# V of a sample in one load of full rows, and the sample steps of the attention at other heads

## The chip, the cores and the metric

The kernel runs on all 8 cores of one Trainium2 chip. Each core has five engines with queues of their own: TensorE (PE, matrix products into PSUM), VectorE (DVE), ScalarE (ACT), GpSimd (POOL, here used for issuing DMAs that convert float32 to bfloat16) and SyncE (SP, which issues the other DMAs). They meet through semaphores alone. The metric is the device time of the slowest core, in microseconds (us), as the median of several runs.

## The reference, cut to what matters

A two-layer decoder trunk runs one step for a prompt group (8 sequences of 2048 tokens) and a sample group (128 sequences of one token, each with its own cached K and V of 256 memory rows). Both share all weights.

```python
def mem_attend(u, k, v, w_q, w_o):
    q = jnp.einsum('btd,de->bte', u, w_q).reshape(b, t, MEM_HEADS, MEM_HEAD_DIM)
    s = jnp.einsum('bthd,bnhd->bhtn', q, k).astype(jnp.float32) * (MEM_HEAD_DIM ** -0.5)
    p = jax.nn.softmax(s, axis=-1).astype(v.dtype)
    o = jnp.einsum('bhtn,bnhd->bthd', p, v).reshape(b, t, d)
    return jnp.einsum('btd,de->bte', o, w_o)
...
        x = x + y
        x = x + mem_attend(rmsnorm(x, g_attn[i]), mem_k[i], mem_v[i], w_q[i], w_o[i])
        x = x + sq_relu_mlp(rmsnorm(x, g_ffn[i]), w_up[i], w_down[i])
```

The width is 1024, there are 4 heads of 256, and 256 memory rows. The change is in `mem_attend` of the sample group, which is worked off inside the prompt group's attention.

## The kernel before, in words

Each core takes one prompt sequence (2048 tokens) and 16 samples, side by side as 2064 columns in five tiles: four of 416 columns and one, tile 4, of 384 prompt columns and the 16 samples. The order of instructions on each engine is the order in which the program is written; a tracker adds the semaphore waits that data, SBUF ranges and PSUM banks ask for. All helpers record on a line of their own: L284 is nearly every matrix product (`mm`), L301 an activation on ACT, L313 a scalar_tensor_tensor on DVE (here the products of a norm, x times gain times reciprocal root), L317 a tensor_tensor on DVE, L331 a copy on DVE, L329 a copy on ACT, L337 a multiply with a sum on DVE (the sample scores), L344 every DMA.

`layer` does the attention first. Its outer loop runs over k = 0..4, the tiles in the order `seq = [0, 4, 1, 2, 3]`; its inner loop runs over the heads h = 0..3, written here as (k, h). In a head stand `S` (scores of the next head, two PSUM banks, exponentials on ACT), a share of the list `big`, `PVh` (weights times V, three banks, normalised by two tensor_tensor on DVE) and the rest of that share. `big` holds `Qgroup(k+1, ec)`, eight products for one 128-column group of Q of the next tile, copied out by ACT, and `Ogroup`, eight products of the output map, added to x by DVE. Products take one of seven banks in turn (`nxt`), so a product waits until what was written seven allocations earlier has been read.

A norm of a tile to come (`norm_t`) stands after `PVh` of head 2 (of head 3 where k is 4): eight products with ones, two activations, and eight DVE products. Only the norm of k = 0 is deferred (`late_n`): its eight DVE products are let out two at a time by `norm_step(2)`, after each entry of `big` in k = 1, and `Qgroup(2, 0)`, the fifth entry there, reads their results.

The 16 samples are steps of a pipeline, one per call of `slot()`, made at the heads in the list `slots`, then once beside the last `Ogroup`s, then in the MLP. Call i runs `SE(i-1)` (exponential on ACT, a copy into a padded matrix on DVE), `SB(i-2)` (four products of 512 columns with V into bank 7), `SDV(i)` (loads V of sample i through POOL) and `SA(i)` (eight L337 on DVE: q times K, summed, for two K tiles of 128 memory rows). Each half of `SA` is followed by the load of a K tile into the buffer just read, `SDK`, three tiles ahead of it, so tile 2b+3 is asked for in the middle of `SA(b)` and read in the second half of `SA(b+1)`. q of the samples is made once, at (0, 2): `sample_q` turns it round on PE, stores it to memory (`qd`), and loads it back as a row repeated over all partitions (`SDQ`), two steps ahead.

At (3, 2) `wrelease_spread` starts a load of the first MLP down weights in eight pieces, one per head (`wspread_step`), on POOL's queue.

Of the kernel before, what the change touches and what calls it, by code (L numbers as in the profile page):

```python
# [8 lines left out]
BF16 = mybir.dt.bfloat16  # L9
# [4 lines left out]
PE, ACT, DVE, POOL, SP = "pe", "act", "dve", "pool", "sp"  # L14
NCORES = 8
D = 1024
# [8 lines left out]
PZM = 66  # L25
# [107 lines left out]
def build_program():  # L133
    nc = bass.Bass("TRN2", target_bir_lowering=False)
    P = Prog()

    def din(name, shape):
        return nc.dram_tensor(name, list(shape), F32, kind="ExternalInput").ap()
# [9 lines left out]
    cv_d = din("cv", [2, NS, NMEM, D])  # L148
# [29 lines left out]
    def DV(ap):  # L178
        return V(ap, [])
# [53 lines left out]
    def sl(a, b):  # L233
        return slice(a, b)

    def PSv(bank, a, b, m=128):
        return V(PS[0:m, bank, a:b], [(PSB + bank * 2048, PSB + (bank + 1) * 2048)], excl=True)
# [45 lines left out]
    def mm(out, lhsT, rhs, start, stop):  # L283
        P.add(PE, "c", lambda e, o=out.ap, l=lhsT.ap, r=rhs.ap: e.matmul(out=o, lhsT=l, rhs=r, start=start, stop=stop),  # L284
              [lhsT, rhs], [out])
# [57 lines left out]
    def dma(q, out, in_, chan, after=()):  # L343
        P.add(q, "d", lambda e, o=out.ap, i=in_.ap: e.dma_start(out=o, in_=i), [in_], [out], chan=chan, after=after)  # L344
# [497 lines left out]
    def layer(l, side=None, tail=None):  # L842
        fin = l == 1
        bank_mod[0] = 7
        s2 = Scratch2()
# [8 lines left out]
        so = s2.top  # L854
        assert so == ZOFF
        KS = [s2.alloc(F32, [D]) for _ in range(3)]
        VS = [s2.alloc(BF16, [2, 512]) for _ in range(4)]
        QB = [s2.alloc(BF16, [D]) for _ in range(2)]
        QS = QB[0]
        PZ = [s2.alloc(BF16, [4, PZW]) for _ in range(2)]  # L860
# [10 lines left out]
        def norm_t(ti, grow, defer=None):  # L871
            c0, n, npmt, ns = TILES[ti]
            norm_b(c0, n, grow, lambda c, c0=c0, n=n: U3(c, sl(c0, c0 + n)), SQ, RSTD, defer=defer)
# [60 lines left out]
                                       [(QDB + 8192 + l * 4096, QDB + 12288 + l * 4096)]), f"qb{b % 2}")  # L934

        def SDV(b):
            for hf in range(2):
                i = (2 * b + hf) % 4
                dma(POOL, VS[i](), DV(cv_d[l, b].rearrange("(nc p) e -> p nc e", p=128)[:, :, hf * 512:(hf + 1) * 512]), f"vs{i}")

        def SA(b):
            for ncx in range(2):
# [12 lines left out]
        def SB(b):  # L955
            for ncx in range(2):
                for hf in range(2):
                    w0 = 64 - (hf * 32 + 2 * b)
                    mm(PSv(7, 0, 512, m=PZM), PZ[b % 2](ncx * 2 + hf, sl(w0, w0 + PZM)), VS[(2 * b + hf) % 4](ncx),
                       b == 0 and ncx == 0 and hf == 0, b == NS - 1 and ncx == 1 and hf == 1)  # L960

        sctr = [0]
# [1 line left out]
        def slot():  # L964
            i = sctr[0]
            sctr[0] += 1
            if 0 <= i - 1 < NS:
                SE(i - 1)
            if 0 <= i - 2 < NS:
                SB(i - 2)  # L970
            if i < NS:
                SDV(i)
                SA(i)
# [28 lines left out]
        for ec in range(NCH):  # L1002
            Qgroup(0, ec)
            if ec == 3:
                norm_t(seq[1], R_ATTN + l)
        slots = [(0, 3), (1, 1), (1, 2), (1, 3), (2, 1), (2, 2), (2, 3), (3, 1), (3, 2), (3, 3), (4, 1), (4, 2)]
        late_n = []

        def norm_step(m):
# [193 lines left out]
    def tail0(j):  # L1203
# [7 lines left out]
        if j in (16, 18):  # L1211
            for half in range(2):
                conv.na((j - 16) // 2, half)
            conv.nb((j - 16) // 2)

    layer(0, side0, tail0)
    bank_mod[0] = 8
    conv.run()
    layer(1)

    sems = {e: es.enter_context(nc.semaphore(f"s_{e}")) for e in (PE, ACT, DVE, POOL)}
# [119 lines left out]
```

How the kernel before makes its waits and increments, by code:

```python
    def emit(name, e):  # L1230
        known = {}
        for op in P.q[name]:
            for d in op.cwaits:
                key = ("e", d.eng)
                if known.get(key, 0) < d.val:
                    e.wait_ge(sems[d.eng], d.val)
                    known[key] = d.val
            for ch, val in op.dwaits:
                key = ("c", ch)
                if known.get(key, 0) < val:
                    e.wait_ge(chans[ch], val)
                    known[key] = val
            ins = op.fn(e)
            if op.kind == "d":
                ins.then_inc(chans[op.chan], 16)
            elif op.sig:
                ins.then_inc(sems[name], 1)
        if name == SP:
            for ch, cnt in P.chan_count.items():
                if known.get(("c", ch), 0) < cnt * 16:
                    e.wait_ge(chans[ch], cnt * 16)
```

## Time and profile before

| | us |
|---|---|
| median of 3 runs | 1636.65 (1635.66 to 1760.3) |
| the profiled execution | 1635.83 |
| its slowest core, first to last instruction (core 4) | 1634.3 |
| its fastest core (core 7) | 1630.4 |
| PE busy on core 4 | 1589.7 |

The profile shows the slowest core of one execution; some 1.5 us lie around its span. PE busy counts stretches in which some matmul is in flight, so a PE at half clock counts as busy too. Layer 0's attention lies at about 95 to 260 us of the span, layer 1's at about 980 to 1137 us.

### The profile page before, as it was taken

What the parts mean: (1) busy time and instruction counts of PE and PEld (TensorE: products, weight loads), DVE (VectorE), ACT (ScalarE), POOL (GpSimd) and SP (SyncE); (2) the same over time, 40 slices, a digit from 0 to 9 for tenths busy, and PEclk for the clock granted to TensorE, in tenths of its full rate; (3) what the DMA queues carried; (4) which work ended last, traced back from release to release, by engine and by line L of the source; (5) the groups of instructions that cost most, each with busy time, mean ns of one, the idle gap of its engine ahead of it and who ended that gap; (6) DMA issues with size and microseconds to landing.
All of it is one profiled execution on the core that took longest, in us unless ns stands there. A gap on an engine that the chain in (4) does not pass through costs nothing.

```text
span 1634.3 us, 27613 instructions; the slowest of 8 cores (1630.4 to 1634.3 us)
## 1 busy us (share of the span) xinstructions
PE 1589.7 (97%) x9490; PEld 911.6 (56%) x9500; DVE 879.5 (54%) x1987; ACT 511.6 (31%) x988; POOL 80.4 (5%) x117
## 2 busy tenths in 40 slices
PE   6898999999999999999999999999999999999997
PEld 5654555555555555555555555555555555555565
DVE  5656577554443444456666572777744444444455
ACT  4755633221221221223222126553311122211234
POOL 0010121000000000000000000121100000000000
PEclk9999999999999999999999999999999999999999
DMA  9996998236307334114000067699406303303013
GB/s 246 195 206 117 211 186 184 73 53 103 59 7 123 66 64 73 32 26 79 1 1 1 1 92 145 155 209 220 112 14 104 52 1 52 52 1 53 21 65 125
DMA packets 70388, 146.20 MB, mean 89 GB/s; under 512 B 4414, under 2 KB 22078, under 8 KB 70236
## 3 DMA queue, kind: packets, MB, share of 16 engines
q0 software_dynamic: 47184, 76.21, 31.2%
q1 hardware_dynamic: 23068, 68.23, 13.5%
q8 instruction: 80, 1.31, 0.3%
q14 instruction: 56, 0.46, 0.1%
HBM read 207.18 MB, written 14.42 MB: 136 GB/s over the span
## 4 chain that ended last, share of the span: by engine, by line
PE 92%; DVE 3%; DMA 2%; ACT 2%; issue 1%; DVEq 0%; ACTq 0%; SPq 0%
PE PS L284 89%; DVE MEM L313 2%; PE PS L288 2%; PE PS L293 1%; ACT MEM L304 1%; DMA MEM<-ck 1%; ACT MEM L301 1%; DMA mn<-MEM 0%; DMA MEM<-qd 0%; DVE MEM L317 0%; DVE MEM L337 0%; DVE MEM L331 0%; ACT MEM L329 0%; DMA MEM<-gv 0%; DMA qd<-MEM 0%
## 5 line engine op out<-in xcount | busy, mean ns | idle before, releaser
L284 PE MATMUL PS<-MEM 128*128 128x416 bf16 (+4 forms) x8578 | 1520.4, 339 | 22.1 <-DVE MEM L317 8.4
L284 PEld LDWEIGHTS PS<-MEM 128*128 128x128 bf16 (+1 forms) x8588 | 841.1, 98 | 689.9 <-issue 35.7
L317 DVE TENSOR_TENSOR MEM<-PS,MEM 128x416 f32<-128x416 f32 (+5 forms) x601 | 339.4, 583 | 318.2 <-PE PS L284 266.7
L301 ACT ACTIVATE MEM<-PS 128x416 f32<-128x416 f32 (+3 forms) x465 | 233.8, 515 | 635.4 <-PE PS L284 537.5
L317 DVE TENSOR_TENSOR MEM<-MEM 128x416 bf16<-128x416 f32 (+1 forms) x320 | 186.4, 587 | 257.5 <-ACT MEM L301 257.5
L313 DVE SCALAR_TENSOR_TENSOR MEM<-MEM 128x416 bf16<-128x416 f32 (+5 forms) x314 | 192.0, 658 | 90.2 <-ACT MEM L301 85.2
L301 ACT ACTIVATE MEM<-MEM 128x1 f32<-128x1 f32 (+7 forms) x201 | 125.5, 633 | 97.1 <-DVE MEM L317 83.6
L337 DVE SCALAR_TENSOR_TENSOR MEM<-MEM 128x256 f32<-128x256 f32 x256 | 91.6, 419 | 20.6 <-DMA MEM<-ck 13.6
L329 ACT COPY MEM<-PS 128x416 f32<-128x416 f32 (+4 forms) x68 | 36.8, 543 | 178.8 <-PE PS L284 158.8
L329 ACT CAST MEM<-PS 128x416 bf16<-128x416 f32 (+3 forms) x101 | 51.9, 516 | 67.4 <-PE PS L284 55.7
L301 ACT ACTIVATE PS<-PS 128x416 f32<-128x416 f32 (+2 forms) x65 | 33.0, 507 | 92.2 <-PE PS L284 92.2
L344 POOL DMA_DIRECT2D MEM<-cv x64 | 44.9, 708 | 329.1 <-PE PS L284 328.7
L288 PE MATMUL PS<-MEM 128*128 128x128 bf16 (+3 forms) x640 | 45.9, 230 | 13.1 <-DVE MEM L313 8.3
L288 PEld LDWEIGHTS PS<-MEM 128*128 128x128 bf16 (+1 forms) x640 | 43.3, 112 | 16.3 <-issue 15.0
L313 DVE SCALAR_TENSOR_TENSOR MEM<-PS,MEM 128x1024 f32<-128x1024 f32 (+2 forms) x20 | 25.6, 1280 | 25.9 <-ACT MEM L301 25.9
L293 PE MATMUL PS<-MEM 128*128 128x128 f32 (+8 forms) x272 | 33.7, 265 | 0.7 <-DVE MEM L313 0.5
L293 PEld LDWEIGHTS PS<-MEM 128*128 128x128 f32 (+8 forms) x272 | 28.2, 130 | 7.5 <-issue 4.0
L304 ACT ACTIVATE MEM<-PS 128x1024 bf16<-128x1024 f32 (+2 forms) x20 | 20.4, 1018 | 34.5 <-PE PS L293 34.5
L344 POOL DMA_DIRECT2D MEM<-w_down x22 | 14.0, 650 | 313.4 <-PE PS L284 231.4
L331 DVE COPY MEM<-PS 128x512 f32<-128x512 f32 (+6 forms) x30 | 19.2, 663 | 15.7 <-PE PS L284 5.4
L304 ACT ACTIVATE MEM<-MEM 128x1024 bf16<-128x1024 f32 (+1 forms) x19 | 20.0, 1054 | 7.8 <-DMA MEM<-x 7.8
L331 DVE COPY MEM<-MEM 128x2 f32<-128x2 f32 (+2 forms) x120 | 15.9, 162 | 9.5 <-ACT MEM L301 9.3
(26 smaller groups left out, 86.5 us busy)
## 6 DMA issues: line engine op xcount, KB each, us to landing
MEM<-ck SPq DMA_DIRECT2D x64, 512.0 KB, 8.3
MEM<-w_up POOLq DMA_DIRECT2D x8, 2048.0 KB, 17.3
MEM<-cv POOLq DMA_DIRECT2D x64, 256.0 KB, 8.8
MEM<-w_down POOLq DMA_DIRECT2D x6, 2048.0 KB, 17.2
MEM<-x SPq DMA_DIRECT2D x16, 512.0 KB, 11.4
MEM<-w_kv POOLq DMA_DIRECT2D x4, 2048.0 KB, 30.2
MEM<-qd SPq DMA_DIRECT2D x32, 256.0 KB, 8.2
y<-MEM SPq DMA_DIRECT2D x15, 512.0 KB, 2.6
```

The lines of the kernel that those rows point to most:

```text
L284: P.add(PE, "c", lambda e, o=out.ap, l=lhsT.ap, r=rhs.ap: e.matmul(out=o, lhsT=l, rhs=r, start=start, stop=stop), [lhsT, rhs], [out])
L288: P.add(PE, "c", lambda e, o=out.ap, l=lhsT.ap, r=rhs.ap: e.matmul(out=o, lhsT=l, rhs=r, start=start, stop=stop, is_transpose=is_transpose ...
L293: P.add(PE, "c", lambda e, o=out.ap, i=in_.ap, d=ident.ap: e.transpose(out=o, in_=i, identity=d), [in_, ident], [out])
L301: P.add(ACT, "c", lambda e, o=out.ap, i=in_.ap: e.activation(out=o, in_=i, func=func, bias=bias, scale=sc), rd, [out])
L304: P.add(ACT, "c", lambda e, o=out.ap, i=in_.ap, c=acc.ap: e.activation(out=o, in_=i, func=func, bias=0.0, scale=1.0, accum_out=c), [in_], ...
L313: P.add(eng, "c", lambda e, o=out.ap, a=in0.ap, b=in1.ap: e.scalar_tensor_tensor(out=o, in0=a, scalar=sc, in1=b, op0=op0, op1=op1), rd, [out])
L317: P.add(eng, "c", lambda e, o=out.ap, a=in0.ap, b=in1.ap: e.tensor_tensor(out=o, in0=a, in1=b, op=op), [in0, in1], [out])
L329: P.add(ACT, "c", lambda e, o=out.ap, i=in_.ap: e.copy(out=o, in_=i), [in_], [out])
L331: P.add(eng, "c", lambda e, o=out.ap, i=in_.ap: e.tensor_copy(out=o, in_=i), [in_], [out])
L337: P.add(DVE, "c", lambda e, o=out.ap, a=in0.ap, b=in1.ap, c=acc.ap: e.scalar_tensor_tensor(out=o, in0=a, scalar=1.0, in1=b, op0=ALU.mult, ...
L344: P.add(q, "d", lambda e, o=out.ap, i=in_.ap: e.dma_start(out=o, in_=i), [in_], [out], chan=chan, after=after)
```

## The change

V of a sample was loaded in two DMAs of 512 columns each, into four buffers of 2 x 512; it is now loaded in one DMA of all 1024 columns, into two buffers of 2 x 1024. The memory used is the same, and V of samples i and i+1 are still held side by side. The list of heads that call `slot()` loses (0, 3), (1, 2), (2, 2) and (3, 2) and gains (1, 0), (2, 0), (3, 0) and (4, 0); it still has 12 entries.

```diff
-        VS = [s2.alloc(BF16, [2, 512]) for _ in range(4)]
+        VS = [s2.alloc(BF16, [2, D]) for _ in range(2)]
...
         def SDV(b):
-            for hf in range(2):
-                i = (2 * b + hf) % 4
-                dma(POOL, VS[i](), DV(cv_d[l, b].rearrange("(nc p) e -> p nc e", p=128)[:, :, hf * 512:(hf + 1) * 512]), f"vs{i}")
+            dma(POOL, VS[b % 2](), DV(cv_d[l, b].rearrange("(nc p) e -> p nc e", p=128)), f"vs{b % 2}")
...
-                    mm(PSv(7, 0, 512, m=PZM), PZ[b % 2](ncx * 2 + hf, sl(w0, w0 + PZM)), VS[(2 * b + hf) % 4](ncx),
+                    mm(PSv(7, 0, 512, m=PZM), PZ[b % 2](ncx * 2 + hf, sl(w0, w0 + PZM)), VS[b % 2](ncx, sl(hf * 512, (hf + 1) * 512)),
...
-        slots = [(0, 3), (1, 1), (1, 2), (1, 3), (2, 1), (2, 2), (2, 3), (3, 1), (3, 2), (3, 3), (4, 1), (4, 2)]
+        slots = [(k, h) for k in range(1, 5) for h in range(4) if h != (3 if k == 4 else 2)]
```

As steps, counted from 0: before, step 0 stood at (0, 3), steps 1 to 3 at heads 1, 2, 3 of k = 1, and so on to steps 10 and 11 at (4, 1) and (4, 2). Now steps 0 to 2 stand at heads 0, 1, 3 of k = 1, 3 to 5 at those of k = 2, 6 to 8 at those of k = 3, and 9 to 11 at heads 0, 1, 2 of k = 4. Steps 1, 4, 7, 10 and 11 stay where they were; the others come one head later.

On DVE, at the passage from k = 0 to k = 1 of a layer, before: the eight L317 are the normalisations of tile 0, L337 is `SA(0)`, each lone L317 of 128x416 with the pair of L313 behind it is one `Ogroup` addition and two products of the deferred norm, and the 128x384 are the normalisations of (1, 0).

```order
L317 TENSOR_TENSOR MEM<-PS,MEM 128x416 x8
L337 SCALAR_TENSOR_TENSOR MEM<-MEM 128x256 x8
L317 TENSOR_TENSOR MEM<-PS,MEM 128x416
L313 SCALAR_TENSOR_TENSOR MEM<-MEM 128x416 x2
L317 TENSOR_TENSOR MEM<-PS,MEM 128x384 x2
L317 TENSOR_TENSOR MEM<-PS,MEM 128x416
L313 SCALAR_TENSOR_TENSOR MEM<-MEM 128x416 x2
L317 TENSOR_TENSOR MEM<-PS,MEM 128x416
L313 SCALAR_TENSOR_TENSOR MEM<-MEM 128x416 x2
L317 TENSOR_TENSOR MEM<-PS,MEM 128x416
L313 SCALAR_TENSOR_TENSOR MEM<-MEM 128x416 x2
```

The same place on DVE now.

```order
L317 TENSOR_TENSOR MEM<-PS,MEM 128x416 x9
L313 SCALAR_TENSOR_TENSOR MEM<-MEM 128x416 x2
L317 TENSOR_TENSOR MEM<-PS,MEM 128x384 x2
L317 TENSOR_TENSOR MEM<-PS,MEM 128x416
L313 SCALAR_TENSOR_TENSOR MEM<-MEM 128x416 x2
L317 TENSOR_TENSOR MEM<-PS,MEM 128x416
L313 SCALAR_TENSOR_TENSOR MEM<-MEM 128x416 x2
L337 SCALAR_TENSOR_TENSOR MEM<-MEM 128x256 x8
L317 TENSOR_TENSOR MEM<-PS,MEM 128x416
L313 SCALAR_TENSOR_TENSOR MEM<-MEM 128x416 x2
```

`SA(0)` moved from ahead of all four pairs of norm products to a place between the third pair and the fourth.

On DVE, from the norm at (3, 2) to (4, 2), before: L313 x8 is that norm, L331 is the copy of `SE`, the three L337 rows are steps 9, 10 and 11 with step 8 ahead of them.

```order
L313 SCALAR_TENSOR_TENSOR MEM<-MEM 128x416 x8
L317 TENSOR_TENSOR MEM<-PS,MEM 128x416
L331 COPY MEM<-MEM 128x4x2
L337 SCALAR_TENSOR_TENSOR MEM<-MEM 128x256 x8
L317 TENSOR_TENSOR MEM<-PS,MEM 128x416 x5
L331 COPY MEM<-MEM 128x4x2
L337 SCALAR_TENSOR_TENSOR MEM<-MEM 128x256 x8
L317 TENSOR_TENSOR MEM<-PS,MEM 128x416 x10
L331 COPY MEM<-MEM 128x4x2
L337 SCALAR_TENSOR_TENSOR MEM<-MEM 128x256 x8
L317 TENSOR_TENSOR MEM<-PS,MEM 128x416 x5
```

The same place on DVE now.

```order
L313 SCALAR_TENSOR_TENSOR MEM<-MEM 128x416 x8
L317 TENSOR_TENSOR MEM<-PS,MEM 128x416 x6
L331 COPY MEM<-MEM 128x4x2
L337 SCALAR_TENSOR_TENSOR MEM<-MEM 128x256 x8
L317 TENSOR_TENSOR MEM<-PS,MEM 128x416 x5
L331 COPY MEM<-MEM 128x4x2
L337 SCALAR_TENSOR_TENSOR MEM<-MEM 128x256 x8
L317 TENSOR_TENSOR MEM<-PS,MEM 128x416 x5
L331 COPY MEM<-MEM 128x4x2
L337 SCALAR_TENSOR_TENSOR MEM<-MEM 128x256 x8
L317 TENSOR_TENSOR MEM<-PS,MEM 128x416 x5
```

Step 8 moved from one tensor_tensor behind the norm to six behind it, and step 9 into the stretch that had ten tensor_tensor in a row; in k = 4 three steps now stand five tensor_tensor apart.

## Rows read from the trace of the kernel before

**Rows 1.** The page: busy time of each engine, share of the span, instructions.

```profile
PE 1589.7 (97%) x9490; PEld 911.6 (56%) x9500; DVE 879.5 (54%) x1987; ACT 511.6 (31%) x988; POOL 80.4 (5%) x117
```

**Rows 2.** Span and mean granted clock of another core.

```profile
core 3: 1634.0 us, clock 0.994
```

**Rows 3.** Core 4, busy time by engine in stretches; then granted clock, DMA share, GB/s.

```profile
126.00:148.00 22.00, 17.44 (x93) 8.87 (x92) 13.38 (x36) 11.14 (x19) 0.00 (x0) 0.92 0.47 106
205.00:235.00 30.00, 27.47 (x146) 14.64 (x144) 21.03 (x71) 10.93 (x23) 5.21 (x9) 0.94 1.01 194
228.40:231.80 3.40, 3.40 (x12) 1.50 (x10) 1.95 (x4) 0.52 (x1) 0.00 (x0) 0.51 1.03 203
1005.00:1032.00 27.00, 22.88 (x133) 12.00 (x131) 15.15 (x42) 15.47 (x30) 0.00 (x0) 1.00 0.29 80
```

**Rows 4.** Core 4, timeline of layer 0's first heads; idle before and releaser in brackets.

```profile
129.57 0.33 SPq L344 DMA_DIRECT2D qd<-MEM  x1
...
134.09 0.49 ACT L301 ACTIVATE MEM<-PS 128x384 f32<-128x384 f32 x1
136.19 0.42 DVE L337 SCALAR_TENSOR_TENSOR MEM<-MEM 128x256 f32<-128x256 f32 x1 [4.31 <-DMA MEM<-qd]
...
138.97 0.58 DVE L317 TENSOR_TENSOR MEM<-PS,MEM 128x416 f32<-128x416 f32 x1
139.47 1.20 DVE L313 SCALAR_TENSOR_TENSOR MEM<-MEM 128x416 bf16<-128x416 f32 x2
...
139.70 5.63 PE L284 MATMUL PS<-MEM 128*128 128x384 bf16 x22 [3.21 <-DVE MEM L317]
...
146.62 18.55 PE L284 MATMUL PS<-MEM 128*128 128x416 bf16 x104 [0.23 <-DVE MEM L313]
```

**Rows 5.** Core 4, timeline of layer 1's first heads.

```profile
1013.40 0.33 SPq L344 DMA_DIRECT2D qd<-MEM  x1
...
1028.78 21.54 PE L284 MATMUL PS<-MEM 128*128 128x416 bf16 x121 [0.23 <-DVE MEM L313]
```

**Rows 6.** Core 3, timeline at the same two places and at (3, 3) of layer 0.

```profile
131.53 0.33 SPq L344 DMA_DIRECT2D qd<-MEM  x1
...
149.23 3.10 PE L284 MATMUL PS<-MEM 128*128 128x416 bf16 x17 [0.23 <-DVE MEM L313]
...
228.92 11.40 PE L284 MATMUL PS<-MEM 128*128 128x416 bf16 x63 [0.92 <-DVE MEM L317]
...
1012.72 0.33 SPq L344 DMA_DIRECT2D qd<-MEM  x1
...
1028.45 6.88 PE L284 MATMUL PS<-MEM 128*128 128x416 bf16 x39 [0.23 <-DVE MEM L313]
```

**Rows 7.** Core 4, timeline around (3, 3) of layer 0.

```profile
216.47 1.71 SPq L344 DMA_DIRECT2D MEM<-ck  x2
...
225.80 0.43 DVE L337 SCALAR_TENSOR_TENSOR MEM<-MEM 128x256 f32<-128x256 f32 x1 [4.08 <-DMA MEM<-ck]
...
227.92 9.39 PE L284 MATMUL PS<-MEM 128*128 128x416 bf16 x42 [2.53 <-DVE MEM L317]
```

**Rows 8.** K tiles from issue to landing, 205 to 250 us and 1085 to 1130 us.

```profile
DMA to landing us min/median/max: 6.2/9.6/11.3
DMA to landing us min/median/max: 5.8/8.1/10.7
```

**Rows 9.** DMA queues: 205 to 250 us (two rows), 1146 to 1180 us, 480 to 700 us.

```profile
q0 software_dynamic: 2863, 3.26, 57.1%
q1 hardware_dynamic: 1753, 5.36, 42.0%
q0 software_dynamic: 1992, 1.91, 37.9%
q0 software_dynamic: 6240, 12.58, 37.2%
```

## The prediction

> **What bounds the kernel now.** The page is read first: PE is busy for 1589.7 of 1634.3 us [rows 1], so nearly all time is matmul time, which the change leaves as it is. What can move is the 44.6 us in which PE does nothing, and stretches at half clock, which count as busy. The second view, PE's waits and the stretches by engine, says which of this lies where steps move. In 126 to 148 us of layer 0 PE is busy 17.44 of 22 us at a mean clock of 0.92; in 205 to 235 us 27.47 of 30 at 0.94; in 1005 to 1032 us 22.88 of 27 at 1.00 [rows 3]. The rest of the attention has no PE wait worth a term. So three places carry the sum, and together they are some 15 us, under one per cent.
>
> The third view, the timeline, tells why. At the first place `SA(0)` stands on DVE ahead of the `Ogroup` additions and of the deferred norm, and waits 4.31 us for the samples' q, which has just gone to memory and back. Behind it PE finds a bank whose addition is queued on DVE and stands for 3.21 us [rows 4]. It comes back to a steady run only at 146.62, when the last norm product lets `Qgroup(2, 0)` finish. Layer 1 has the same shape with a faster return of q [rows 5], and so has core 3 [rows 6]. At the second place, (3, 3) of layer 0, step 9 follows step 8 so closely that its second K tile, asked for at 216.47, is not there until 225.80; DVE waits 4.08 us, PE stands 2.53 us [rows 7] and then runs 3.4 us at a granted clock of 0.51, the lower of its two levels (1.2 of 2.4 GHz) [rows 3]. On core 3 this place costs 0.92 us [rows 6].
>
> **The change, part by part.** The sum is made for core 3, at 1634.0 us [rows 2], since core 4, at 1634.3, owes 4.2 us to the second place alone and falls behind it when that goes. The profiled execution took 1635.83, so 1.5 lie around the slowest span; it is 0.8 under the median of the runs shown.
>
> *Step 0 to (1, 0), first place.* From the end of `SA(0)` at 138.97 to the resumption of Q at 146.62 DVE works off four additions, four pairs of norm products and two normalisations: 7.65 us. An addition with its pair takes 0.50 and 1.20 [rows 4]. Now the first addition with its pair (1.7) fits into what was the wait for q, from 131.88 on. The normalisations of (1, 0) need the reciprocals, which end at 134.58 [rows 4]. From there the other 5.95 us and `SA(0)` itself, 2.78 (136.19 to 138.97), must pass before the last norm product, since `SA(0)` stands ahead of the last pair: 134.6 + 8.7 = 143.3. So Q resumes 13.75 us after the store of q at 129.57, where it took 17.05. q lands before `SA(0)` wants it, near 139. With 13.75 at all four places, core 4 gains 3.3 in layer 0 and 1.6 in layer 1, core 3 4.0 and 2.0 [rows 4 to 6]. Had `SA(0)` stood behind all eight products, it would be 2.8 us more each time; the list names heads that hold no norm, yet the deferred norm of k = 0 lies in head 0 and head 1 of k = 1.
>
> *The clock there.* PE will reach the seventh product of `Qgroup(2, 0)` some 2.4 us before DVE does. Standing still for 2.53 us was followed by a half-clock stretch of 3.4 us on core 4 [rows 3, 7], which costs 1.7; in layer 1 shorter pauses left it at 1.00 [rows 3]. So 0 to 3.4 for two layers; I take 1.7, since 2.4 is nearer to 2.53 than to the pauses that cost nothing.
>
> *Steps 2, 3, 5, 6, 8 and 9 one head later.* Each takes its `SE`, `SB`, V load and K loads along. A head of k = 1 or 2 with a step has 38 products (24 in groups, 4 of `S`, 6 of `PVh`, 4 of `SB`), at 18.55 / 104 = 0.178 us each [rows 4] 6.8 us. Step 9 no longer follows 8 within a few us, so the stall at (3, 3) goes: 0.9 on core 3, 2.5 and 1.7 of clock on core 4 [rows 3, 6, 7]. The norms at head 2 start with DVE free of a step; nothing on PE waited for them, so that is worth nothing.
>
> *What is late next: k = 4.* It gets three steps where it had two. DVE carries it: eight products of scores (2.8), a copy (0.2) and five tensor_tensor (2.6) are 5.6 us against PE's 6.8 per head. What does not carry it is DMA, which is full from 205 to 235 us (share 1.01) [rows 3]. Over 205 to 250 us 99% of 16 engines' time went into five steps and eight pieces of weights [rows 9]. A piece is 128 packets of 2 KB at 210 ns (37.2% of 220 us x 16 / 6240 [rows 9]), 1.7 us; so a step costs (44.6 - 13.4) / 5 = 6.2 us. Between the start of step 8 and the tile that step 11 reads last, steps 8 and 9, V and a K tile of step 10 and four pieces must move: 12.4 + 4.5 + 6.8 = 23.7 us. From (3, 3) to (4, 2) PE has 42 + 38 + 38 products, 21.1 us, and the first half of `SA(11)` adds 1.4. With the time that any K tile takes to land (5.8 at the least [rows 8], of which transfer is the smaller part), step 11 waits for K for 1 to 6 us. I take 4.0 in layer 0, the wait that the same crowding gave at (3, 3) [rows 7], and 2.5 in layer 1, where K lands 1.5 us sooner (8.1 against 9.6 in the median [rows 8]). Behind `SA(11)` on DVE are the addition of `Ogroup` 9, the normalisations of (4, 3) and the norm; PE has 42 products, 7.5 us, before it takes that addition's bank again. DVE's own share of that is 0.6 for the addition ahead, 3.0 for the step, 0.6 for the addition behind it and about 1.1 carried over from step 10, so it bears a wait of 2.2: PE stalls 1.8 and 0.5 us, together 2.3. Bounds: 0, if both waits stay under 2.2, and 9, if both are 6 (3.8 each, with a half clock once).
>
> *V in whole rows.* Half as many issues on POOL, which is busy for 5% of the span [rows 1]. In DMA time 512 packets at 103 ns (37.9% of 34 us x 16 / 1992 [rows 9]), 3.3 us, become 256 at the 210 ns of the weights' rows, 3.4 us: nothing. `SB` reads V two steps on; the closest is now step 9, asked for at (4, 0) and read at (4, 2), 13.6 us later, where two steps were as close before. I count 0, and up to 2 against it if that load is among the late ones. Nor does POOL's order hurt: the pieces of weights now stand one ahead of the V load of steps 8 to 11, one short issue each on an engine that waits for PE there anyway.
>
> **Sum.** Core 3: 1634.0 - 4.0 - 2.0 - 0.9 + 1.7 + 2.3 = 1631.1. Core 4 comes to 1634.3 - 3.3 - 1.6 - 4.2 + 4.0 = 1629.2. The slowest plus 1.5 gives 1632.6; I say 1633, three under the profiled execution. A measurement of this kernel tells 2%, 33 us, from no change; no mechanism here is of that size.
>
> **Rivals.**
> *V's long rows hold K back (slower).* K tiles (SP's queue) and V (POOL's) share the 16 engines. If each record of a K tile waits its turn behind one of V, then the 8 records per engine of a tile wait 8 x (210 - 103) ns = 0.9 us longer each time [rows 9]. Steps 10 and 11 are each 0.9 later, which is 1.7 more stall in layer 0, 1.7 in layer 1 and the half clock once: 1632.6 + 5.1 = 1637.7. It decides from a median landing of K above 10.5 us in k = 4. For it speaks that K's landings already rise from 6.2 to 11.3 with V beside them [rows 8]; against it, that the same bytes need the same time. The Trainium skill, "DMA: Bandwidth & Descriptors", section "Queues, rings and completion order", has the rule behind this: each engine takes turns between queues by packets, not by bytes. By that rule the longer rows shift the share of an engine to V; no row of before separates it from plain crowding.
> *A clean gain.* K waits in k = 4 stay under what DVE bears and the clock does not fall: 1634.0 - 6.9 + 1.5 = 1628.6. For it speaks that (4, 1) and (4, 2), also 38 products apart, had no PE wait.
> *The new wait takes the old one's place.* Steps are only shifted: half clock in both layers (3.4) and a stall in k = 4 like that at (3, 3) in both (2.5 each) give 1634.0 - 6.9 + 8.4 + 1.5 = 1637.0, on core 3, no change that could be told.
>
> **Chances.** Forecast 0.5, held-back K 0.15, clean gain 0.2, exchanged waits 0.15. The range goes from a little below the clean gain, 1628, to a little over the rivals at the upper end, 1640. Faster by over 2% 0.01, within 2% 0.98, slower by over 2% 0.01.
>
> **What would show it.** Right: no DVE wait for q at step 0 and none of 3 us on PE near 140 us; PE waiting instead 2 to 3 us for a norm product (DVE L313) before `Qgroup(2, 0)`; no wait of PE between 148 and 225 us in layer 0; a DVE wait for K of 2 to 5 us at (4, 1) or (4, 2) and a PE wait behind it; twice as few V packets at the same DMA share. Wrong: a PE wait for V itself, K waits over 6 us, DVE late at heads 0 and 1 of k = 2 or 3, where I expect nothing, or half-clock stretches at places not named.

## The result, and the profile after

The kernel after took 1648.16 us (median; the kernel before 1636.16 in the same comparison), a ratio of 1.0069, 95% interval 1.0057 to 1.0080. That is no change by the 2% bound, but it is a loss of 11 to 12 us where three were to be gained, and it lies outside the forecast range, 1628 to 1640. The profiled execution of after took 1648.71 us.

The first view is the span and granted clock of each core:

```profile
core 0: 1641.6 us, clock 0.992
core 1: 1630.7 us, clock 0.996
core 2: 1630.7 us, clock 0.995
core 3: 1645.1 us, clock 0.992
core 4: 1628.6 us, clock 0.996
core 5: 1643.5 us, clock 0.991
core 6: 1639.1 us, clock 0.994
core 7: 1646.6 us, clock 0.990
```

Three cores (1, 2, 4) run about as forecast; five are 6.5 to 16.2 us longer than before, and the slowest sets the time. Before, all eight lay between 1630.4 and 1634.3, and core 7 was the quickest.

The page's line on the engines, which answers to [rows 1], counts the loss only in part, since time at half clock (the lower of PE's two levels, 1.2 of 2.4 GHz) is busy time:

```profile
PE 1596.2 (97%) x9500; PEld 914.2 (56%) x9500; DVE 879.6 (53%) x1987; ACT 511.9 (31%) x988; POOL 58.0 (4%) x85
```

Stretches of core 7, then of core 4, and last of core 7 before, show where it is (length, PE busy, granted clock, DMA share, GB/s):

```profile
120.00:150.00 30.00, 26.68 (x149) 0.94 0.51 105
212.00:262.00 50.00, 44.63 (x237) 0.97 1.01 215
1000.00:1033.00 33.00, 29.94 (x170) 0.95 0.44 103
1100.00:1150.00 50.00, 43.58 (x229) 0.93 1.00 203
...
212.00:262.00 50.00, 48.78 (x274) 1.00 0.97 220
1100.00:1150.00 50.00, 50.00 (x282) 1.00 0.99 236
...
120.00:150.00 30.00, 25.16 (x146) 1.00 0.51 105
212.00:262.00 50.00, 50.00 (x283) 1.00 1.03 218
1000.00:1033.00 33.00, 28.52 (x166) 1.00 0.26 81
1100.00:1150.00 50.00, 50.00 (x283) 1.00 0.99 211
```

What a stretch loses is its length less busy time times clock. On core 7 k = 4 loses 50 - 44.63 x 0.97 = 6.7 us in layer 0 and 50 - 43.58 x 0.93 = 9.5 in layer 1, together 16.2, as much as its span grew, 1646.6 - 1630.4; before, PE of that core was busy for all 50 us of both stretches at 1.00. On core 4 the same places lose 1.2 and 0. The first place loses 4.9 and 4.6 on core 7, and lost 4.8 and 4.5 before: nothing won there.

The timeline of core 7 at the first place answers to [rows 4 to 6] (start, duration, instruction; idle before and its releaser in brackets):

```profile
131.07 0.33 SPq L344 DMA_DIRECT2D qd<-MEM  x1
...
132.25 9.44 PE L284 MATMUL PS<-MEM 128*128 128x416 bf16 x54 [0.34 <-ACT MEM L301]
144.44 0.34 PE L284 MATMUL PS<-MEM 128*128 128x416 bf16 x1 [2.75 <-DVE MEM L313]
145.00 5.30 PE L284 MATMUL PS<-MEM 128*128 128x416 bf16 x20 [0.23 <-DVE MEM L313]
```

Q resumes 145.00 - 131.07 = 13.93 us after the store of q, where 13.75 was forecast, and behind a wait of 2.75 for a norm product, as forecast. But 20 products follow in 5.30 us instead of 3.6: the half clock follows the wait.

In k = 4 the waits of DVE for DMA on core 7 answer to [rows 7], and then those of PE:

```profile
231.53 0.42 DVE L337 SCALAR_TENSOR_TENSOR MEM<-MEM 128x256 f32<-128x256 f32 x1 [4.38 <-DMA MEM<-ck]
237.23 0.42 DVE L337 SCALAR_TENSOR_TENSOR MEM<-MEM 128x256 f32<-128x256 f32 x1 [1.67 <-DMA MEM<-qd]
240.10 0.43 DVE L337 SCALAR_TENSOR_TENSOR MEM<-MEM 128x256 f32<-128x256 f32 x1 [1.40 <-DMA MEM<-ck]
245.87 0.42 DVE L337 SCALAR_TENSOR_TENSOR MEM<-MEM 128x256 f32<-128x256 f32 x1 [1.73 <-DMA MEM<-qd]
249.34 0.42 DVE L337 SCALAR_TENSOR_TENSOR MEM<-MEM 128x256 f32<-128x256 f32 x1 [2.00 <-DMA MEM<-ck]
...
240.56 7.71 PE L284 MATMUL PS<-MEM 128*66 128x512 bf16 x42 [1.13 <-DMA MEM<-cv]
251.46 10.73 PE L284 MATMUL PS<-MEM 128*128 128x416 bf16 x50 [3.19 <-DVE MEM L317]
...
1123.76 7.71 PE L284 MATMUL PS<-MEM 128*66 128x512 bf16 x42 [0.71 <-DMA MEM<-cv]
1137.17 13.00 PE L284 MATMUL PS<-MEM 128*128 128x416 bf16 x58 [5.71 <-DVE MEM L317]
```

The first row is step 9 at (4, 0), the next two pairs are steps 10 and 11, each late by q and by K, and these waits add up on DVE. PE meets them as V that is not there (128*66 is `SB`) and, at the end of k = 4, as a bank whose addition (L317) stands behind the scores on DVE. The 50 products after 251.46 take 10.73 us instead of 8.9, and the 58 after 1137.17 take 13.00 instead of 10.3: half clock again.

The DMA queues of core 7 from 205 to 250 us and its K tiles there, from issue to landing, answer to [rows 9] and [rows 8]:

```profile
q0 software_dynamic: 1838, 3.48, 53.4%
q1 hardware_dynamic: 2027, 6.26, 47.2%
...
DMA to landing us min/median/max: 9.5/10.5/13.9
```

They move 9.74 MB in 45 us, 216 GB/s, with the engines full.

### The profile page after: what moved, and what is told of

Its sections match the earlier page's. It is cut to its first block, busy times and chain, and to the rows that moved or that the text cites. A ratio compares the mean times of both kernels' runs of the same rounds, so it can differ in the third digit from the quotient of the medians.

```text
span 1646.6 us, 27501 instructions; the slowest of 8 cores (1628.6 to 1646.6 us)
## 1 busy us (share of the span) xinstructions
PE 1596.2 (97%) x9500; PEld 914.2 (56%) x9500; DVE 879.6 (53%) x1987; ACT 511.9 (31%) x988; POOL 58.0 (4%) x85
## 4 chain that ended last, share of the span: by engine, by line
PE 89%; DMA 4%; DVE 4%; ACT 2%; issue 1%; DVEq 0%; SPq 0%; ACTq 0%
PE PS L284 86%; PE PS L288 2%; DMA MEM<-ck 2%; DVE MEM L313 2%; DMA MEM<-qd 2%; PE PS L293 1%; DVE MEM L337 1%; DVE MEM L317 1%; ACT MEM L304 1%; ACT MEM L301 1%; DMA mn<-MEM 0%; DVE MEM L331 0%; DMA MEM<-gv 0%; ACT MEM L329 0%; ACT PS L301 0%
## 5 line engine op out<-in xcount | busy, mean ns | idle before, releaser
L284 PEld LDWEIGHTS PS<-MEM 128*128 128x128 bf16 (+2 forms) x8588 | 842.2, 98 | 700.0 <-issue 47.4
L317 DVE TENSOR_TENSOR MEM<-PS,MEM 128x416 f32<-128x416 f32 (+5 forms) x601 | 338.6, 583 | 305.4 <-PE PS L284 259.2
L317 DVE TENSOR_TENSOR MEM<-MEM 128x416 bf16<-128x416 f32 (+1 forms) x320 | 186.5, 588 | 257.5 <-ACT MEM L301 257.5
L313 DVE SCALAR_TENSOR_TENSOR MEM<-MEM 128x416 bf16<-128x416 f32 (+5 forms) x314 | 192.0, 658 | 89.2 <-ACT MEM L301 83.9
L337 DVE SCALAR_TENSOR_TENSOR MEM<-MEM 128x256 f32<-128x256 f32 x256 | 91.9, 419 | 35.8 <-DMA MEM<-ck 27.4
L288 PEld LDWEIGHTS PS<-MEM 128*128 128x128 bf16 (+1 forms) x640 | 44.8, 114 | 15.6 <-issue 14.3
L313 DVE SCALAR_TENSOR_TENSOR MEM<-PS,MEM 128x1024 f32<-128x1024 f32 (+2 forms) x20 | 25.6, 1281 | 26.3 <-ACT MEM L301 26.3
L344 POOL DMA_DIRECT2D MEM<-cv x32 | 22.5, 703 | 354.4 <-PE PS L284 354.4
L331 DVE COPY MEM<-PS 128x512 f32<-128x512 f32 (+6 forms) x30 | 19.2, 663 | 16.1 <-PE PS L288 6.7
L331 DVE COPY MEM<-MEM 128x2 f32<-128x2 f32 (+2 forms) x120 | 15.9, 163 | 19.3 <-ACT MEM L301 19.3
```

The source lines that it names most:

```text
L313: P.add(eng, "c", lambda e, o=out.ap, a=in0.ap, b=in1.ap: e.scalar_tensor_tensor(out=o, in0=a, scalar=sc, in1=b, op0=op0, op1=op1), rd, [out])
L317: P.add(eng, "c", lambda e, o=out.ap, a=in0.ap, b=in1.ap: e.tensor_tensor(out=o, in0=a, in1=b, op=op), [in0, in1], [out])
L331: P.add(eng, "c", lambda e, o=out.ap, i=in_.ap: e.tensor_copy(out=o, in_=i), [in_], [out])
L337: P.add(DVE, "c", lambda e, o=out.ap, a=in0.ap, b=in1.ap, c=acc.ap: e.scalar_tensor_tensor(out=o, in0=a, scalar=1.0, in1=b, op0=ALU.mult, ...
```

## The experiments

Two theories could make K and V late. Theory 1: (3, 3), (4, 0), (4, 1) and (4, 2) are four heads in a row with a step, 6.8 us apart, and ask for more than DMA brings. Theory 2: V's rows of 2 KB push K's transfers back. Theory 3 puts the loss on step 0's new place. All runs were compared with the kernel before on the same chip (medians 1635.84 to 1637.59); ratios are to it.

**The list alone, and V alone.** The change was taken apart. The first kernel has the new list with V in halves, the second the old list with V whole.

```diff
 # e1_slots_only: before, with
-        slots = [(0, 3), (1, 1), (1, 2), (1, 3), (2, 1), (2, 2), (2, 3), (3, 1), (3, 2), (3, 3), (4, 1), (4, 2)]
+        slots = [(k, h) for k in range(1, 5) for h in range(4) if h != (3 if k == 4 else 2)]
 # e2_vwhole_only: after, with
-        slots = [(k, h) for k in range(1, 5) for h in range(4) if h != (3 if k == 4 else 2)]
+        slots = [(0, 3), (1, 1), (1, 2), (1, 3), (2, 1), (2, 2), (2, 3), (3, 1), (3, 2), (3, 3), (4, 1), (4, 2)]
```

> The kernel before with the new list of steps alone; V stays in halves. Theory 1 (three steps in k = 4 meet a full DMA, so K, V and q land late): the loss stays, 1645 to 1649, with the waits of the kernel after at (4, 0) to (4, 2). Theory 2 (V's long rows hold K back): the loss is gone, 1633 to 1637, and K in k = 4 lands in the median under 10 us. Theory 3 (the wait and the half clock at step 0's new place): the loss stays, 1645 or more, but the waits in k = 4 need not.

> The kernel after with the old list of steps; V whole alone. Theory 1: as the kernel before, 1634 to 1638. Theory 2: most of the loss, 1642 or more, with K in 205 to 250 us landing later than before on the slowest core. Theory 3: as the kernel before, 1634 to 1638, the old wait for q back at (0, 3).

The list alone took 1641.87 us (ratio 1.0040, 1.0026 to 1.0054), V alone 1641.30 (1.0035, 1.0021 to 1.0048). Neither theory had this: each part costs about half, 6.0 and 5.5, and the sum, 11.5, is nearly all of the 12.0 that the whole change costs. (The 6.0 is what is left after the gain of step 0's new place, which is measured alone below.) The trace tells what differs. PE's waits from 205 to 262 us on the slowest core with the list alone (core 3), then the landings of K there from 205 to 250 us:

```profile
PE PS L284 <- DMA MEM<-cv: 3.8, 1, 3.8
...
DMA to landing us min/median/max: 7.6/9.3/10.7
```

The same for core 3 of after, K's landings alone (its slowest core, 7, had 10.5 in the median, above):

```profile
DMA to landing us min/median/max: 8.2/12.1/14.0
```

With halves K comes in 9.3 us and DVE bears its waits; it is V that is late, and PE waits for V itself. With whole rows K takes 12.1, and PE waits behind DVE instead. So V's rows decide what is late. It does not take the new list for that: with the old list and V whole, PE waits behind DVE too, for up to 2.6 us from 205 to 262 us and for 0.7 to 3.8 from 1093 to 1155 us, and on no core for V.

**V whole rows, in two loads.** This tells the length of the rows from the size of one load.

```diff
-        VS = [s2.alloc(BF16, [2, D]) for _ in range(2)]
+        VS = [s2.alloc(BF16, [D]) for _ in range(4)]
...
-            dma(POOL, VS[b % 2](), DV(cv_d[l, b].rearrange("(nc p) e -> p nc e", p=128)), f"vs{b % 2}")
+            for ncx in range(2):
+                i = (2 * b + ncx) % 4
+                dma(POOL, VS[i](), DV(cv_d[l, b].rearrange("(nc p) e -> p nc e", p=128)[:, ncx]), f"vs{i}")
```

> The kernel after, but V of a sample comes in two loads of 128 whole rows each instead of one of 256. If it is the length of the rows (2 KB packets taking turns with K's) that makes K late in the kernel after, this is like it: 1646 to 1650, PE waiting for DVE L317 by 3 us or more in k = 4 and hardly for V. If it is that one load carries all of V, this is like the run with the new list and halves: 1640 to 1643, PE waiting for V by 2 to 4 us instead.

It took 1654.19 us (1.0104, 1.0089 to 1.0118), worse than after and above both ranges that were expected. On its slowest core, 6, PE waits like this from 205 to 262 us, and K lands like this from 205 to 250 us:

```profile
PE PS L284 <- DVE MEM L317: 6.7, 2, 4.2
PE PS L284 <- DMA MEM<-cv: 0.2, 1, 0.2
...
DMA to landing us min/median/max: 8.6/12.9/14.4
```

So it is the rows: same loads and bytes as with halves, rows of 2 KB instead of 1 KB, and K's median on the slowest core goes from 9.3 to 12.9. Over all eight cores the medians are 8.9 to 10.2 with the list alone, 9.7 to 12.1 in after and 9.6 to 12.9 here. The Trainium skill, "DMA: Bandwidth & Descriptors", section "Queues, rings and completion order", says that an engine takes turns between its queues by packets; a packet there is made of several descriptors. These landings agree with turns that grow with the rows, but no run shows how V's rows are packed. Theory 2 stands, as one half: that long rows make K late is shown, that the turns are the reason is argued. Why two loads are worse than one by some 6 us was not tried.

**Less traffic in k = 4.** Three kernels keep whole rows and take traffic away there: the weight pieces come later, the list has one step less in k = 4 (the last then runs behind the attention), or V is not loaded from the third sample on.

```diff
 # e3_late_weights
-                if (k, h) == (3, 2):
+                if (k, h) == (4, 3):
                     wrelease_spread(f"wq{l}")
 # e4_two_in_k4
-        slots = [(k, h) for k in range(1, 5) for h in range(4) if h != (3 if k == 4 else 2)]
+        slots = [(k, h) for k in range(1, 5) for h in range(4) if h != 2 and (k < 4 or h == 1)] + [(4, 2)]
...
-            if c == 3 and sctr[0] < NS + 2:
+            if (c == 3 or (c == 5 and sctr[0] == NS + 1)) and sctr[0] < NS + 2:
 # e10_no_v_loads, in SDV
+            if b < 2:
-            dma(POOL, VS[b % 2](), DV(cv_d[l, b].rearrange("(nc p) e -> p nc e", p=128)), f"vs{b % 2}")
+                dma(POOL, VS[b % 2](), DV(cv_d[l, b].rearrange("(nc p) e -> p nc e", p=128)), f"vs{b % 2}")
```

> The kernel after, but the spreading of the weight pieces begins after head (4, 3) instead of (3, 2), so that three steps in k = 4 share DMA with no weights. Theory 1: 1630 to 1636, if the weights still come before they are read; PE's waits for DVE L317 and for V in 215 to 255 us gone. Theory 2: V's rows still meet K's, 1642 to 1648. Theory 3: the wait for L313 and the half clock near 146 us stay and so does the time, 1643 to 1648.

> The kernel after with heads 1 and 2 of k = 4 alone as places, eleven in all; the last step runs behind the attention. Theory 1: most of the loss gone, 1631 to 1637, if the step behind the attention costs under 2 us per layer. Theory 2: V's rows are as long, so 1641 or more. Theory 3: step 0 is where it was in the kernel after, so 1643 or more.

> The kernel after without the loads of V from the third sample on; V of the first two samples is used again in their place, all else is done. A step then moves 1.31 instead of 1.84 MB, at 216 GB/s 6.1 instead of 8.5 us, under the 6.8 between steps. Theory 1: the loss is gone although the weights still come there, 1630 to 1636, K waits on DVE in k = 4 under 2 us. If the three steps load DVE or PE's order too much, whatever DMA brings, it stays: 1643 or more.

Late weights: 1638.80 us (1.0016, 1.0006 to 1.0026). In layer 0 no core loses over 0.8 us in k = 4; in layer 1 four still lose 3 to 7, and a fifth 2. Core 2, the same two stretches as of core 7 above:

```profile
212.00:262.00 50.00, 49.19 (x274) 1.00 0.98 212
1100.00:1150.00 50.00, 46.78 (x248) 0.93 1.03 212
```

The expected 1630 to 1636 was missed by 3. Four steps in a row fill DMA without any weights: from 1103 to 1119 us of core 2, ahead of the first piece, its share is 1.01, and at 1115.94 DVE has waited 3.21 us for K of step 10. But POOL waits for nothing there and issues four pieces at 1119.23, so this run does not tell what they add to PE's wait of 3.22 us, which ends at 1127.82. One step less in k = 4: 1633.98 us (0.9989, 0.9980 to 0.9998), with whole rows and the weights where they were. Without V's loads: 1633.33 us (0.9979, 0.9970 to 0.9988), with four steps in a row and the weights; waits of DVE for K from 205 to 262 us are 0.5 to 2.3 in all there, where core 7 of after had 12.3. Core 7 of each, the same two stretches, first with one step less, then without V:

```profile
212.00:262.00 50.00, 49.19 (x274) 1.00 0.93 199
1100.00:1150.00 50.00, 50.00 (x283) 1.00 1.01 194
...
212.00:262.00 50.00, 50.00 (x281) 1.00 0.81 175
1100.00:1150.00 50.00, 50.00 (x282) 1.00 0.62 161
```

The work of three steps on DVE and PE does fit into k = 4; their bytes do not. DMA's share alone doesn't tell this: 1.01 with one step less in layer 1, and no loss.

**Whole rows or halves where DMA keeps up.** V's three places of the diff above were set back to halves in the kernel with one step less.

> The run with two places in k = 4, with V in halves again. Theory 1 (V's rows only decide who loses when four steps in a row ask for more than DMA brings): the same as that run within 2 us, 1632 to 1636. Theory 2 (long rows cost by themselves): 3 or more below it, under 1631.

1633.71 us (0.9982, 0.9973 to 0.9991) against 1633.98 with whole rows: the same. Long rows cost nothing here that could be told; the cost came where transfers are late already.

**Step 0's place.** The list of before with the place of step 0 alone moved; then, in the kernel with one step less, three norm products behind each group instead of two, with whole rows and with halves.

```diff
 # e11_step0_only: before, with
-        slots = [(0, 3), (1, 1), (1, 2), (1, 3), (2, 1), (2, 2), (2, 3), (3, 1), (3, 2), (3, 3), (4, 1), (4, 2)]
+        slots = [(1, 0), (1, 1), (1, 2), (1, 3), (2, 1), (2, 2), (2, 3), (3, 1), (3, 2), (3, 3), (4, 1), (4, 2)]
 # e7_two_in_k4_norm3 (and e9_norm3_halves, with V in halves), at both calls
-                    norm_step(2)
+                    norm_step(3)
```

> The kernel before with the place of step 0 alone moved, from (0, 3) to (1, 0). By the rows of the kernel after, PE there loses 4.9 per layer (3.3 idle, 1.6 at half clock) where before it lost 4.8 to 7.5 in layer 0 and 4.1 to 5.7 in layer 1, and k = 4 is as before: 1634 to 1637, at most 2 gained. By the prediction's sum, 4.2 are gained (4.0 and 2.0 less 1.7): 1631 to 1633.

> The run with two places in k = 4, and three deferred norm products behind each group of 8 products instead of two, so that all eight products stand ahead of SA(0). If the wait for L313 and the half clock at step 0's place cost what their rows say (2.8 and 1.7 per layer), 9 less than that run less what SA(0) then makes late: 1625 to 1630. If DVE just hands the wait to the next addition, no change: 1632 to 1635.

> Two places in k = 4, three norm products behind each group, and V in halves. If the length of V's rows costs nothing where DMA keeps up, as with the run with two norm products: 1625 to 1627, the same as with whole rows. If whole rows still cost the 0.3 to 0.9 that PE waits for DVE L317 there, 1624 to 1626, not to be told from it.

The place alone: 1634.54 us against 1637.59 (0.9985, 0.9976 to 0.9995), a gain of 0.8 to 3.9 us. That is as the rows of after had it (1634 to 1637) and under the prediction's sum, 4.0 + 2.0 - 1.7 = 4.3 (the expectation wrote 4.2). Theory 3 falls as the cause of the loss: the place loses as much after as before on core 7, and moving it alone gains. With three products: 1626.00 us (0.9934, 0.9921 to 0.9947), halves 1625.17 (0.9935, 0.9921 to 0.9949). What stands ahead of `SA(0)` is the point: two per group put six products ahead of `SA(0)` and the last two behind it, three put all eight ahead. Core 7 of the kernel with three and whole rows, timeline at the first place and then its first stretch:

```profile
132.42 11.53 PE L284 MATMUL PS<-MEM 128*128 128x416 bf16 x66 [0.40 <-ACT MEM L301]
144.56 15.61 PE L284 MATMUL PS<-MEM 128*128 128x384 bf16 x88 [0.61 <-DVE MEM L317]
...
120.00:150.00 30.00, 29.00 (x173) 1.00 0.56 115
```

The stretch loses 1.0 us instead of 4.9, without half clock. These two kernels beat both the kernel before and after, by 11 to 12 and by 22 to 23 us.

## Why the prediction was wrong

The step that failed is the price of k = 4, and in it the sentence "so a step costs (44.6 - 13.4) / 5 = 6.2 us". It put the DMA time of 205 to 250 us on five steps and eight pieces of weights because so many were asked for in it. The packets of core 4 in that stretch say how much was brought:

```profile
DMA packets 4618, 8.65 MB, mean 192 GB/s; under 512 B 382, under 2 KB 2543, under 8 KB 4616
```

The packets of 1 KB, 2543 - 382 = 2161, are V, 512 to a step: 4.2 steps. They hold 2.21 of the 3.26 MB of POOL's queue [rows 9], and the other 1.05 MB are four pieces of 0.262 MB, not eight. The 5.36 MB of SP's queue are two K tiles and q, 1.311 MB a step: 4.1 steps. So a step cost (44.6 - 4 x 1.7) / 4.1 = 9.2 us, of which 4.6 for K and q (42.0% of 45 us, over 4.1) and as much for V. At 6.2 a step fits between two heads 6.8 apart, and a run of them can be kept up; at 9.2 it can't, and every step of the run adds 2.4. The runs agree: without V a step is 4.6 us by the same price, 6.3 with a piece of weights, and the loss is gone; with a gap at (4, 0) it is gone too.

By terms:

- *First place, -4.0 and -2.0, clock +1.7.* The mechanism was right, the resumption within 0.2 us. Of core 3's gain the clock takes back more than the one stretch counted: half clock followed the wait of 2.6 to 2.8 us in 14 of 16 cases (eight cores, two layers), about 1.7 each. Core 3 lost 6.7 and 4.5 there before and 4.9 and 4.9 after (120 to 150 and 1000 to 1045 us): 1.4 won instead of 4.3. The slowest core of after won nothing.
- *(3, 3), -0.9.* Right: DVE of core 7 waits for no K there. At (3, 1), before it, it waits for 4.47 us, and behind that PE stands for 0.45.
- *k = 4, +2.3, bounds 0 to 9.* Mis-sized: 16.2 on core 7, 9.6 + 5.9 on core 3 (212 to 265 and 1093 to 1155 us). With the step at 9.2 us, 4.6 of it for V and 1.8 for a K tile, the transfers counted as 23.7 are 2 x 9.2 + 6.4 + 6.8 = 31.6, an estimate: later by 7.9 in each layer, before any half clock. In layer 0 DVE of core 7 waited 11.2 at steps 9 to 11 (the five rows in the section on the result).
- *V in whole rows, 0.* Wrong where DMA is late: 5.5 alone. With the new list PE met late V itself, 0.4 to 1.5 us in each layer on the five slow cores; the prediction had named that as a sign of being wrong. The rival on V's long rows named the right effect, K held back, and priced it at 5.1; it was given 0.15 because the same bytes need the same time, which is true of their sum and says nothing of who waits.
- *Chances.* That the two came together was no case of its own: forecast and rivals each took one, and the upper end of the range was that of one.

What stays open is why one core of a pair loses and not the other (below).

## What to carry to other kernels

Price a transfer by the bytes that a queue moved in a stretch, not by the transfers that were asked for in it: where landings take longer than the spacing of the issues, the two differ, here by 1.3 times (five steps and eight pieces are 11.3 MB, and 8.6 came). Where DMA is full, a step's spacing must be compared with its bytes before it is moved next to another, and a gap of one head can be worth more than the wait that the move removes. Longer rows of one transfer were free here while DMA kept up (1633.98 against 1633.71 us) and made the other queue's transfers late where it did not.

## What was not expected of the hardware

Cores 0 and 1, 2 and 3, 4 and 5 of after differ by 11 to 15 us with the same program. From 1100 to 1140 us cores 0 to 3 show (busy time, clock, DMA share, GB/s):

```profile
1100.00:1140.00 40.00, 34.85 (x188) 0.96 0.99 202
...
1100.00:1140.00 40.00, 38.23 (x215) 1.00 1.04 250
...
1100.00:1140.00 40.00, 40.00 (x225) 1.00 1.05 243
...
1100.00:1140.00 40.00, 35.82 (x193) 0.97 0.94 199
```

The neighbours together get 452 and 442 GB/s. Before, cores 0 and 1 had these rows there:

```profile
1100.00:1140.00 40.00, 40.00 (x226) 1.00 1.05 231
...
1100.00:1140.00 40.00, 39.33 (x222) 1.00 1.05 219
```

That is 231 + 219 = 450, and cores 2 and 3 had 227 + 221 = 448, near to even, and lost next to nothing. So two neighbours seem to share some 450 GB/s, and where both ask for more one falls behind, with its DMA engines as full (0.94 to 1.05). Which of the two it is changed from run to run (0 and 3 here, 1 and 3 with the list alone); no run told what decides it, and that they share a limit is read from sums, not shown by a run.

PE waits of 2.6 to 2.8 us for a norm product were followed by 1.7 us of lost clock in most cases and not in all; no run told the two apart.
